# Expert query projections as products of split parts, lows on GpSimd, and a later slab fetch

## The reference, cut to what matters

```python
x = x + y                                             # attention output added
x = x + peer_ffn(rms_norm(x, g_ffn), w_peer_q, sub1, sub2, peer_u, peer_v)

def peer_ffn(h, w_q, sub1, sub2, u, v):
    qry = h @ w_q                                     # 1024 -> 8 heads * 256 = 16 tiles of 128
    s1, s2 = scores of the two halves of qry against 128 keys each
    v1, i1 = top_k(s1, 16); v2, i2 = top_k(s2, 16)    # 16 x 16 candidates
    top_s, pos = top_k(cand, 16); gate = softmax(top_s)
    a = gelu(h . u[expert]); return (a * gate) @ v[expert]

mod = cond @ w_ada[l] + b_ada[l]                      # 48 columns a layer, for the second model
```

## Time and profile before

| | us |
|---|---|
| median of three runs | 2125.06 |
| the profiled execution's own time | 2123.53 |
| its span | 2121.7 |
| TensorE matmul busy | 2033.3 (96%) |
| VectorE busy | 1515.4 (71%) |
| ScalarE busy | 1078.5 (51%) |
| GpSimd busy | 208.3 (10%) |

### The profile page before, as it was taken

One profiled execution on the slowest core, in us unless ns is written; L12 is line 12 of the kernel. 1 busy time (PEld: TensorE's weight loads), 2 busy tenths in 40 slices (PEclk: granted clock), 3 DMA queues, 4 the chain that ended last, 5 costly groups with the idle time before them and its releaser, 6 DMA issues.

```text
span 2121.7 us, 44666 instructions
## 1 busy us (share of the span) xinstructions
PE 2033.3 (96%) x15166; PEld 1911.4 (90%) x15166; DVE 1515.4 (71%) x3542; ACT 1078.5 (51%) x2199; POOL 208.3 (10%) x218
## 2 busy tenths in 40 slices
PE   8999999878999999999999999999999999999998
PEld 6757889867999999999989888899998978899998
DVE  5755499597767888888876377776666647777666
ACT  3241266696444444444446455654445655655454
POOL 0000199683000000000000000000000000000000
PEclk9999999999999999999999999999999999999999
DMA  7333545302558777777644543445554553345553
GB/s 300 120 129 129 218 159 178 129 0 71 186 180 296 279 276 272 279 279 269 235 154 165 179 141 108 140 157 181 180 185 134 181 173 110 103 160 176 183 183 109
DMA packets 103246, 375.96 MB, mean 177 GB/s; under 512 B 11473, under 2 KB 11745, under 8 KB 102881
## 3 DMA queue, kind: packets, MB, share of 16 engines
q1 hardware_dynamic: 88992, 323.86, 45.7%
q10 hardware_dynamic: 14144, 50.72, 6.1%
HBM read 373.47 MB, written 1.05 MB: 177 GB/s over the span
## 4 chain that ended last, share of the span: by engine, by line
PE 74%; issue 15%; DVE 5%; POOL 2%; DVEq 1%; ACT 1%; ACTq 0%; POOLq 0%
PE bank L748 22%; PE bank L754 21%; PE bank L751 21%; POOL part_lo L1507 2%; DVE one_hots L1772 2%; PE bank L940 1%; PE bank L896 1%; PE bank L978 1%; DVE part_lo L1924 1%; PE bank L860 1%; PE bank L839 1%; PE bank L866 1%; PE bank L863 1%; DVE arena L2095 1%; DVEq L2094 1%
## 5 line engine op out<-in xcount | busy, mean ns | idle before, releaser
L1188 ACT ACTIVATE part_hi<-ring 128x512 fp32r<-128x512 f32 x1080 | 663.4, 626 | 421.2 <-PE bank L751 397.8
L1788 DVE TENSOR_TENSOR part_lo<-ring,part_hi 128x512 fp32r<-128x512 f32 x684 | 452.2, 688 | 218.4 <-ACT part_hi L1188 213.0
L748 PE MATMUL bank<-u_hi,part_hi 128*128 128x256 f32 (+1 forms) x1792 | 517.8, 289 | 23.6 <-POOL part_lo L1507 12.4
L754 PE MATMUL bank<-u_hi,part_lo 128*128 128x256 f32 (+1 forms) x1792 | 505.1, 282 | 0.0
L751 PE MATMUL bank<-u_lo,part_hi 128*128 128x256 f32 (+1 forms) x1792 | 503.4, 281 | 0.0
L748 PE MATMUL bank<-w_hi,part_hi 128*128 128x256 f32 x1376 | 389.9, 283 | 4.7 <-DVE w_lo L1815 3.3
L751 PE MATMUL bank<-w_lo,part_hi 128*128 128x256 f32 x1376 | 389.2, 283 | 0.0
L754 PE MATMUL bank<-w_hi,part_lo 128*128 128x256 f32 x1376 | 389.1, 283 | 0.0
L748 PEld LDWEIGHTS bank<-u_hi,part_hi 128*128 128x128 f32 (+1 forms) x1792 | 337.3, 188 | 33.5 <-issue 13.6
L754 PEld LDWEIGHTS bank<-u_hi,part_lo 128*128 128x128 f32 (+1 forms) x1792 | 339.9, 190 | 0.5
L751 PEld LDWEIGHTS bank<-u_lo,part_hi 128*128 128x128 f32 (+1 forms) x1792 | 338.1, 189 | 1.3
(11 more groups left out here) (278 smaller groups left out, 2973.5 us busy)
## 6 DMA issues: line engine op xcount, KB each, us to landing
ring<-stream_dram SPq DMA_DIRECT2D x606, 512.0 KB, 3.3
arena<-ada_dram ACTq DMA_DIRECT2D x96, 512.0 KB, 4.6
xT<-x_dram SPq DMA_DIRECT2D x4, 256.0 KB, 5.7
arena<-mem_dram SPq DMA_DIRECT2D x1, 1024.0 KB, 9.6
arena<-keys_dram SPq DMA_DIRECT2D x1, 1024.0 KB, 5.2
out_dram<-uT SPq DMA_DIRECT2D x2, 512.0 KB, 2.6
cst<-consts_dram SPq DMA_DIRECT2D x1, 841.0 KB, 14.4
cond<-cond_dram SPq DMA_DIRECT2D x1, 512.0 KB, 15.2
```

What stands on the lines that cost most here:

```text
L748: m = pe.matmul(o, hi, u(cc), start=first, stop=False, **flags)
L754: m = pe.matmul(o, lo, u(cc), start=False, stop=last, **flags)
L1188: act.activation(part_hi[:, h % 4, 0:width], ring[:, n % RING, (h % 2) * width:(h % 2 + 1) * width], ACT.Copy).then_inc(hi_ready, 1)
L1788: v.tensor_tensor(part_lo[:, h % 4, :], ring[:, n % RING, (h % 2) * 512:(h % 2 + 1) * 512], part_hi[:, h % 4, :], ALU.subtract).then_inc(l ...
```

## The change

Of the sixteen query tiles the first two stay as they are; the other fourteen are computed by `passes` from split parts, like the experts. `u_hi` is now written by ScalarE, chunk by chunk as the normed chunks come; `u_lo` by VectorE in eight chunks, right after the second plain tile (it overwrites `uT`, which the plain tiles read). Each of the fourteen slots is split in two halves by ScalarE between the evictions, and GpSimd writes its 28 low halves. The first four halves of the experts are split behind them in the same sequence, before the keys and right after them, so the count of halves before the experts is 28 instead of 0. The sine and cosine tables move from behind the ninth to behind the seventh query eviction (`j == 6`), the slab fetch to behind the eviction of tile 12 (`j == 12`, tiles counted from 0).

```diff
+PQ_PLAIN = 2
+PQ_HALVES = 2 * (PEER_Q - PQ_PLAIN)
...
             for j in range(PEER_Q):
-                linear(S_PQ + j, T_PQ + j, uT, DC, fresh=(p_normed, 0) if j == 0 else None)
+                if j < PQ_PLAIN:
+                    linear(S_PQ + j, T_PQ + j, uT, DC, fresh=(p_normed, 0) if j == 0 else None)
+                    continue
+                b = free_bank(T_PQ + j)
+                for h in (2 * (j - PQ_PLAIN), 2 * (j - PQ_PLAIN) + 1):
+                    m = passes(h, 0, lambda c: (b[:, 0:S], c == 0, c == DC - 1),
+                               lambda c: u_hi[:, c, :], lambda c: u_lo[:, c, :],
+                               (plo_chunk, 0) if j == PQ_PLAIN else None)
+                m.then_inc(tile_full, 1)
...
             act.wait_ge(p_sum, 1)
             root_of(root[:, 0:S], bank[0][:, 0:S]).then_inc(p_root, 1)
+            for h in range(3):
+                query_half(h)
+            for c in range(DC):
+                act.wait_ge(p_normed, c + 1)
+                act.activation(u_hi[:, c, :], uT[:, c, :], ACT.Copy).then_inc(phi_chunk, 1)
+            query_half(3)
             for j in range(PEER_Q):
+                if j >= 2:
+                    query_half(2 * j)
                 evict(T_PQ + j, qry[:, j, :])
-                if j == 8:
+                if 2 <= j < PEER_Q - 1:
+                    query_half(2 * j + 1)
+                if j == 6:
                     act.wait_ge(turn_ready, 1)
                     act.activation(cosT[:, :], tab[:, 0, :], ACT.Sin)
                     act.activation(sinT[:, :], tab[:, 1, :], ACT.Sin).then_inc(rope_ready, 1)
+                if j == 12:
                     fetch_early(2)
...
-            high_parts(0, 0)
-            high_parts(1, 0)
...
+            for h in range(PQ_HALVES):
+                low_half(S_PQ + PQ_PLAIN + h // 2, h, 0)
...
             v.drain()
-            v.tensor_copy(u_hi[:, :, :], uT[:, :, :])
+            v.wait_ge(tile_full, T_PQ + PQ_PLAIN)
+            for c in range(DC):
+                v.wait_ge(phi_chunk, c + 1)
+                v.tensor_tensor(u_lo[:, c, :], uT[:, c, :], u_hi[:, c, :], ALU.subtract).then_inc(plo_chunk, 1)
...
-            v.wait_ge(tile_full, T_KEYS)
-            v.tensor_tensor(u_lo[:, :, :], uT[:, :, :], u_hi[:, :, :], ALU.subtract).then_inc(usplit_ready, 1)
```

More of the change, by code:

```diff
@@ L68 @@
     int(x) for x in np.cumsum([0, 2 * L_UQ, 48, 24, 16, 6 * FT]))
-assert all(h % 4 == 0 for h in (PEER_HALVES, LH_GATE, LH_WO, LH_OUT, LH_FFN, L_HALVES))
+assert all(h % 4 == 0 for h in (PQ_HALVES, PEER_HALVES, LH_GATE, LH_WO, LH_OUT, LH_FFN, L_HALVES))
 def slot_of_half(h):
@@ L757, in passes @@
                 return m
+            for j in range(PEER_Q):
+                if j < PQ_PLAIN:
[7 more added lines that the diff above has]
+                m.then_inc(tile_full, 1)
+            pe.wait_ge(keys_loaded, 16)
+            pe.wait_ge(tile_out, T_KEYS)
+            for j in range(8):
+                tt, g0 = j // 4, (j % 4) * 4
+                b = free_bank(T_KEYS + j)
+                for g in range(4):
+                    side, h = (g0 + g) // 8, (g0 + g) % 8
+                    m = pe.matmul(b[:, g * P:(g + 1) * P], qry[:, 2 * h + side, tt * P:(tt + 1) * P],
+                                  keysT[:, g0 + g, :], start=True, stop=True)
+                m.then_inc(tile_full, 1)
             def expert_act(i, k, turns, slots=12):
@@ L764, in expert_act @@
                 for h in (2 * k, 2 * k + 1):
-                    m = passes(h, turns * (2 * slots), lambda c: (bank[i % 2][:, 0:S], c == 0, c == DC - 1),
+                    m = passes(h, turns * (2 * slots) + PQ_HALVES, lambda c: (bank[i % 2][:, 0:S], c == 0, c == DC - 1),
                                lambda c: u_hi[:, c, :], lambda c: u_lo[:, c, :])
@@ L1163, in _, with split_half, split_slot, high_parts @@
                 square(sq[:, c, :], xT[:, c, :]).then_inc(p_sq, 1)
+            def split_half(n, h, uses, before, width=512):
+                act.wait_ge(loaded[n % RING], (uses + (n // RING + 1)) * 16)
+                if not isinstance(before, int) or before + h >= 4:
+                    act.wait_ge(half_begun, before + (h - 2))
+                act.activation(part_hi[:, h % 4, 0:width], ring[:, n % RING, (h % 2) * width:(h % 2 + 1) * width],
+                               ACT.Copy).then_inc(hi_ready, 1)
+            def split_slot(n, k, uses, before):
+                for h in (2 * k, 2 * k + 1):
+                    split_half(n, h, uses, before)
+            def high_parts(k, turns, slots=12):
+                split_slot(S_PEER + k, k, turns * (slots // RING), turns * (2 * slots) + PQ_HALVES)
+            def query_half(h):
+                n = S_PQ + PQ_PLAIN + h // 2
+                if h < PQ_HALVES:
+                    split_half(n, h, 0, 0)
+                else:
+                    split_half(n, h - PQ_HALVES, 0, PQ_HALVES)
             act.wait_ge(p_sum, 1)
             root_of(root[:, 0:S], bank[0][:, 0:S]).then_inc(p_root, 1)
+            for h in range(3):
[4 more added lines that the diff above has]
+            query_half(3)
             for j in range(PEER_Q):
+                if j >= 2:
+                    query_half(2 * j)
                 evict(T_PQ + j, qry[:, j, :])
-                if j == 8:
+                if 2 <= j < PEER_Q - 1:
+                    query_half(2 * j + 1)
+                if j == 6:
                     act.wait_ge(turn_ready, 1)
@@ L1181, in gelu @@
                     .then_inc(gelu_done, 1)
-            def split_half(n, h, uses, before, width=512):
-                act.wait_ge(loaded[n % RING], (uses + (n // RING + 1)) * 16)
-                if not isinstance(before, int) or before + h >= 4:
-                    act.wait_ge(half_begun, before + (h - 2))
-                act.activation(part_hi[:, h % 4, 0:width], ring[:, n % RING, (h % 2) * width:(h % 2 + 1) * width],
-                               ACT.Copy).then_inc(hi_ready, 1)
-            def split_slot(n, k, uses, before):
-                for h in (2 * k, 2 * k + 1):
-                    split_half(n, h, uses, before)
-            def high_parts(k, turns, slots=12):
-                split_slot(S_PEER + k, k, turns * (slots // RING), turns * (2 * slots))
+            query_half(2 * PEER_Q - 1)
             act.drain().then_inc(gelu_done, 1)
-            high_parts(0, 0)
-            high_parts(1, 0)
             def column_distance(q, it):
```

29 lines of the change are left out of this document (9 added, 20 removed).

## The result

The changed kernel takes 2130.21 us (median of 12 runs, 2124.29 to 2133.25), the kernel before 2125.39 (12 runs, 2120.56 to 2127.88). The ratio is 1.0023 with an interval of 1.0013 to 1.0032: slower by 4.9 us, a little beyond what I called no change. The forecast was +2.0.

The account below looks back on a forecast made before the run. TensorE bounds the query stage (busy 55.48 of 55.70 us). Gain -12.6, `u_lo` +1.0, angles and slabs +11.1, slow clock +1.7, start +0.8 make +2.0 us: 2127, own range 2123 to 2131, with rivals 2114 to 2131.5.

Parts of the forecast that it names:

- The step on which it rested: Query stage: GpSimd and VectorE block each other, each standing still until the other's instruction is through, modulation's custom instruction included.
- products: Query tiles: a tile of 24 split-part matmuls takes 2.85 instead of 3.47 us; 8.7 us gained over 14 tiles.
- Start: Start of the query stage: three halves meet the normed chunks, costing between 0 and 2.5 us; 0.8 taken.
- Angles: Before tile 9: angle operations pass one per 1.4 us between lows, the cosine waits, GpSimd runs dry; 3.2 us.
- Slabs: Slabs 8 to 15 on VectorE hold up GpSimd's halves; with the angles 11.1 us, plus 1.7 for slow clock.
- two ways: Slabs either hold GpSimd off as a pack, or alternate, each half 2.4 instead of 1.43; both 11.0 to 11.2.
- Slab fetch: Slabs 16 to 23 asked for behind tile 12, about 246.5 instead of 225.7; the last 14 to 21 us later.
- Selection: Starts 7 to 14 us late, adding nothing or little; sign: its wait shrinks from 13.4 to below 7.
- Place of the acts: Sign that the forecast is right: acts start near 263; before 258 would show it wrong.
- The first: Rival: modulation instruction doesn't block GpSimd, only the angles do; 3.2 instead of 11.1, sum -5.9, 2119; chance 0.21.
- the second: Rival: neither angles nor modulation block GpSimd, or VectorE slips into its gaps; -11, 2114; chance 0.12.
- The third: Rival: selection becomes the bound, `top16` starting at 270 or later; late by 18 gives +6.3, 2131; chance 0.20.

Follow-up runs that it names:

- Experiment 3: Changed kernel with the first four high halves split behind the eight `u_hi` chunks on ScalarE, instead of three ahead of them: 2128.47 us, 1.0015 to the kernel before.
- experiment 1: Changed kernel with slabs 8 to 15 reduced on VectorE in the mix stage (output projection), before GpSimd has work: 2125.55 us, 0.9999 to the kernel before.
- Experiment 5: experiment 1 with the sine and cosine tables behind the eviction of tile 13 instead of 6: 2120.73 us, 0.9978 to the kernel before.
- experiment 2: Changed kernel with the slab fetch spread, one issue behind each tile from 8 to 15 instead of eight behind tile 12: 2130.87 us, 1.0031.
- experiment 8: Changed kernel with slabs 8 to 15 reduced by a plain one-input TENSOR_REDUCE, without the product with `cond`: 2125.4 us, 1.0001 to the kernel before.
- experiment 7: Kernel before, queries still float32, with four expert halves split ahead and slabs 8 to 15 reduced in the output projection: 2123.77 us, 0.999.
- experiment 9: Changed kernel with the slab fetch behind the eviction of tile 8 instead of tile 12: 2139.76 us, 1.0062 to the kernel before.
- experiment 6: Experiment 5 plus four halves split behind `u_hi`, fetch spread over tiles 8 to 15, slabs 16 to 23 reduced after the queries: 2117.12 us, 0.9959.
- experiment 4: Kernel before with only the first four expert halves split ahead of the keys: 2123.19 us, 0.9988.

## Why the prediction was right or wrong

The step on which it rested held: GpSimd's lows and VectorE's two-input operations get in each other's way, and that eats the gain. The total came out 3.2 us above the forecast (2130.21 against 2127), in the range and on the slower side. That it came so near is in part luck: the start and the last tiles cost 6.7 more than forecast, the angles and slabs 4.4 less. By the terms of the sum, measured from the first normed chunk to the 24th act half in the profiled executions:

| term | forecast | measured | from |
|---|---|---|---|
| products | -8.7 | -9.0 | tile pitch 2.83 (12 halves from 210.10 to 227.06), 14 tiles |
| gap behind the keys | -2.2 | -2.2 | 0.69 left of 2.88 |
| slow clock behind it | -1.7 | -1.7 | no such stretch there |
| `u_lo` | +1.0 | +0.7 | wait of 0.61, first half 0.08 longer |
| lows among the chunks | +0.8 | +3.3 | below |
| angles and slabs, with slow clock | +12.8 | +8.4 | half 21 at 246.75, due 238.36 |
| last tiles | 0 | +4.2 | keys at 261.37, due 257.15 |
| sum | +2.0 | +3.7 | +3.7 by the two traces |

- **Start: mis-sized.** I took the chunks to go as a pack. Two lows slipped in among them, and the chunks took 2.04 longer. The 3.3 are 1.03 of longer idle time of TensorE, and plain tiles of 9.24 instead of 6.94, with a second wait of 0.43 and a stretch at 1.2 GHz (mean 0.64 from 198 to 202). Experiment 3 gave 1.7 of the 3.3 back; the rest is the clock's.
- **Angles: right, a little over-sized.** Ten operations let through, one per 1.4 us, the cosine late, GpSimd dry, TensorE idle. I had said about 11 us of idle before tile 9; it was 3.30 and the rest came in small parts. Without the slabs, in experiment 1, the angles' stall is 2.31, against the 3.2 of the sum. Experiment 5 took away the wait and left the operations as slow as they were.
- **Slabs: over-sized.** I named two ways and gave both 11. It was turn-taking. But the first slab ran before GpSimd had a half, and the second only held up the first half, within the stall of 3.30. So there were six turns and not eight, and a turn costs 2.22 - 1.41 = 0.81, not 0.97: the measure is TensorE's pitch, not GpSimd's time alone. The stall of 3.30 and six times 0.81 make 8.2 of the 8.4 in the table. So the slow clock behind the stall (mean 0.66 from 232 to 237), which the sum had at 1.7, cost about 0.2: TensorE had time to spare between two lows. Experiment 1 is 4.7 us below the changed kernel.
- **Slab fetch: missed.** The prediction moved the fetch in time and asked only when its data would land. It did not count the eight issues as work of ScalarE: 4.39 us in a queue that owes a half every 1.41. I had seen for the angles that the splits are queued behind a wait of ScalarE, and did not ask it here. The rows had the price: before the change two of the same issues take 0.82, only nobody waited for them. That is the +4.2, together with the slabs 16 and on, which took turns with the last lows (2.14 and 2.29), and a slow stretch (mean 0.57 from 257 to 261, a loss of 1.7). The gap of 1.97 and that loss leave about 0.5 for turns that the gap doesn't hold. How the gap itself divides between hold and turn isn't settled: experiment 2 took away the hold but lengthened the turns.
- **Selection: right.** It starts at 268.14, 13.3 later than before (9.8 from the first normed chunk), within the 7 to 14 forecast. Its slack in the acts was 13.4 before. Now it is 7.7, a little above the "below 7" that I had given as a sign (who, for whom, total, times, longest):

```profile
DVE arena L1788 <- ACT arena L1248: 7.7, 1, 7.7
```

- **Place of the acts.** They were to start near 263; by the trace it was 269.62, 266.2 without the 3.45 that came ahead of the change.
- **Rivals.** The first (the custom instruction doesn't block) and the second (nothing does) fell by the 2.28 and the 1.34 above; experiment 8 shows what the slabs look like when their instruction doesn't block. The third (the selection as the bound) fell by the slack of 7.7.

## What to carry to other kernels

Work moved to GpSimd is paid by VectorE too: list what VectorE does in that stretch that a trace shows slowed beside GpSimd (here operations with two SBUF inputs, and TENSOR_SCALAR and CAST), give each one turn of the other engine, and see who waits for the last of them. Here the same change cost 4.9 us as it stood and gave 8.7 once VectorE's side was cleared and the waits were put behind it; 6.7 of these are the products' (experiment 7). And a transfer issue is an instruction of its engine: eight in a row on the engine that feeds the others are a stall, one by one they held nobody up, and here the eight that had to wait for their buffers (experiment 9) cost more than the same eight issued later.

## What the runs showed of the hardware that I had not expected

- VectorE operations that follow each other without a drain do not keep GpSimd out. They alternate with it: custom reductions of 128 x 1024 1.15 apart alone, 2.22 apart in turns. A plain reduction with one input and the same length isn't touched and touches nothing (1.14 and 1.25). One input alone is no safeguard: the one-input TENSOR_SCALAR of 128 x 256 went from 0.29 to 1.34.
- Eight transfer issues in a row on ScalarE's queue took 4.39 us, 0.55 each; single ones 0.33.
- The stretches at 1.2 GHz are hard to forecast from idle time. They lay behind gaps of 3.30 and 1.97 in the changed kernel. The same gap of 3.00 behind the root had one in experiments 3 (a mean of 0.59 from 194 to 198) and 6 (0.72), and none in the kernel before (1.00). When gaps went, the stretch moved in experiment 4, and one more than counted vanished in experiment 5. So a gap's own length is what I would count on, and about 1.7 us for the clock, more or less, is uncertain.
